# Rows of the first expert pair gathered from DRAM instead of selected on TensorE; sums of the later norms moved to VectorE and GpSimd; two spin counts changed

## The reference

```python
x = _layer_norm(ALPHA * x + gt1 * y, ln_g[l, 0], ln_b[l, 0])
h = x * (1 + sc2) + sh2
y = _hmoe(h, rg_w[l], rg_b[l], re_w[l], re_b[l], exp_wg[l], exp_wu[l], exp_wd[l])
x = _layer_norm(ALPHA * x + gt2 * y, ln_g[l, 1], ln_b[l, 1])

def _hmoe(...):           # comb: weight of each expert for each token, zero but for two
    hid = silu(einsum('nd,edf->nef', xf, wg)) * einsum('nd,edf->nef', xf, wu)
    hid = hid * comb[:, :, None]
    return einsum('nef,efd->nd', hid, wd)
```

## Time and profile before

| | |
|---|---|
| median of three executions | 1046.03 us (1041.26 to 1055.11) |
| the profiled execution, its own time | 1048.08 us |
| its span, first to last instruction | 1046.4 us |
| mean granted TensorE clock | 0.937 of 2.4 GHz |
| TensorE (PE) busy | 917.7 us, 88% |
| VectorE (DVE), ScalarE (ACT), GpSimd (POOL) busy | 31%, 22%, 17% |

### The profile page before, as it was taken

How to read it: one execution, slowest core, us unless ns; L and a number is a source line. 1 busy time by engine, 2 the same in 40 slices (tenths; PEclk the granted TensorE clock), 3 DMA queues, 4 the chain that set the end, 5 groups by cost and what they waited for, 6 DMA issues and landing times.

```text
span 1046.4 us, 19214 instructions
## 1 busy us (share of the span) xinstructions
PE 917.7 (88%) x8268; PEld 627.0 (60%) x8268; DVE 327.6 (31%) x841; ACT 232.0 (22%) x528; POOL 177.2 (17%) x230
## 2 busy tenths in 40 slices
PE   2799999889988989999787899898899989997874
PEld 0477667869876757655354567554467757553442
DVE  0523341535425454211123301221221354211134
ACT  0312225223215041111001332221222131110004
POOL 0100002011542151221031110000000233211122
PEclk9899989999998998999996999899889998999996
DMA  9742221340246931799959454555646724899931
GB/s 385 322 152 89 81 81 48 127 163 4 85 173 271 387 139 57 277 425 423 424 194 369 194 189 179 195 196 214 243 164 234 322 97 182 328 424 421 383 110 46
DMA packets 28773, 230.14 MB, mean 220 GB/s; under 512 B 6590, under 2 KB 7006, under 8 KB 13552
## 3 DMA queue, kind: packets, MB, share of 16 engines
q1 hardware_dynamic: 19200, 208.66, 49.8%
q0 software_dynamic: 7776, 15.50, 4.2%
q10 hardware_dynamic: 1712, 4.75, 1.3%
HBM read 222.16 MB, written 16.32 MB: 228 GB/s over the span
## 4 chain that ended last, share of the span: by engine, by line
PE 68%; DMA 19%; DVE 5%; issue 3%; ACT 2%; POOL 1%; SPq 1%; ACTq 0%; POOLq 0%; DVEq 0%
PE ps L646 21%; PE ps L984 10%; DMA arena<-in_w 8%; DMA arena<-in_experts 6%; PE ps L772 5%; PE ps L667 5%; PE ps L1040 4%; PE ps L628 3%; PE ps L779 3%; DMA arena<-zbuf 2%; PE ps L1005 2%; DMA ring<-in_w 2%; PE ps L1154 2%; PE ps L970 1%; PE ps L925 1%
## 5 line engine op out<-in xcount | busy, mean ns | idle before, releaser
L646 PE MATMUL ps<-arena,ring 128*128 128x288 f32 x896 | 230.9, 420 | 11.5 <-DVE arena L1471 3.8
L646 PEld LDWEIGHTS ps<-arena,ring 128*128 128x128 f32 x896 | 173.9, 196 | 68.9 <-issue 17.1
L984 PE MATMUL ps<-arena 128*64 128x256 f32 x960 | 118.6, 404 | 18.0 <-DMA arena<-in_experts 12.6
L984 PEld LDWEIGHTS ps<-arena 128*64 128x64 f32 x960 | 75.0, 146 | 60.8 <-DMA arena<-in_experts 17.8
L667 PE MATMUL ps<-arena,csil 128*32 128x512 f32 x256 | 40.1, 756 | 36.8 <-DMA arena<-in_w 36.8
L772 PE MATMUL ps<-arena 64*64 64x64 f32 x1888 | 63.8, 221 | 4.3 <-issue 3.2
L772 PEld LDWEIGHTS ps<-arena 64*64 64x64 f32 x1888 | 60.3, 137 | 10.2 <-issue 8.5
L628 PEld LDWEIGHTS ps<-con,arena 128*128 128x128 f32 (+3 forms) x270 | 34.5, 149 | 45.5 <-issue 26.6
L628 PE MATMUL ps<-con,arena 128*128 128x128 f32 (+3 forms) x270 | 52.5, 309 | 10.2 <-DVEq L1737 6.3
L1040 PE MATMUL ps<-arena 128*64 128x512 f32 x208 | 58.4, 598 | 0.8 <-DVE arena L1678 0.8
L2003 ACT ACTIVATE arena<-ps 128x128 f32<-128x128 f32 x36 | 10.0, 277 | 208.8 <-PE ps L984 208.8
(11 more groups left out here) (306 smaller groups left out, 1270.3 us busy)
## 6 DMA issues: line engine op xcount, KB each, us to landing
arena<-in_experts SPq DMA_DIRECT2D x30, 2048.0 KB, 20.6
ring<-in_w SPq DMA_DIRECT2D x24, 2048.0 KB, 8.4
arena<-in_w SPq DMA_DIRECT2D x16, 2048.0 KB, 13.3
arena<-in_experts SPq DMA_DIRECT2D x30, 1024.0 KB, 19.3
ring<-in_experts SPq DMA_DIRECT2D x6, 2048.0 KB, 19.8
ring<-in_experts SPq DMA_DIRECT2D x6, 1024.0 KB, 16.5
arena<-in_lora SPq DMA_DIRECT2D x1, 2560.0 KB, 40.8
hbuf<-arena SPq DMA_DIRECT2D x4, 512.0 KB, 3.2
```

What stands on the lines that cost most here:

```text
L646: last = mm(ps[:, tile % 4, 0:T], wslot[j][:, k, o * P:(o + 1) * P], rhs_at(k), start=k == 0, stop=k == KT - 1)
L984: last = mm(ps[64 * j:64 * j + 64, 2 + b, 0:256], x(k), ewgu[slot][:, k, j * 256:(j + 1) * 256], start=k == 0, stop=k == KT - 1)
```

## The change

Three parts, in both layers.

1. **First pair.** `first_rows` is gone. `fetch(0)` gathers the pair's rows like every other pair's. TensorE runs `tables(0)`, the count, `tables(1)`, `spin(2, 3)`, `step_t(0)` (which waits for the gather), then expert 0; `step_t(1)` moves ahead of expert 1. GpSimd fetches pairs 0 and 1 ahead of `places()` and 2 and 3 behind it. `xsel` moves onto `htok`, `ysel` away from it.
2. **Norms 1 and 3.** VectorE sums the tiles in `residual`, GpSimd the squares, as for norms 0 and 2; TensorE's six products of squares between the transposes become one product with the sum. The addition of the two result rows is split: VectorE adds the first two quarters (after `z_in0`), GpSimd the last two (after `z_in1`, new semaphore `zsum2`).
3. **Spins.** Ahead of the transposes 30 products in place of 24, ahead of K 8 in place of 5.

```diff
@@ TensorE, layer_norm @@
-                if n % 2:
-                    add_squares(n, KT - 2)
                 pe.wait_ge(s["ln_sum"], n + 1)
                 mm(ps[:, 4, 0:T], co("mean"), zsum_, start=True, stop=False)
...
-                if not n % 2:
-                    pe.wait_ge(s["ln_ssum"], n // 2 + 1)
-                    mm(ps[:, 5, 0:T], co("mean"), ssum, start=True, stop=False)
-                add_squares(n, KT - 1).then_inc(s["ln_var"], 1)
+                pe.wait_ge(s["ln_ssum"], n + 1)
+                mm(ps[:, 5, 0:T], co("mean"), ssum, start=True, stop=False)
+                pe.wait_ge(s["ln_sq"], KT * (n + 1))
+                mm(ps[:, 5, 0:T], co("mean"), acts(SQB[n])[:, KT - 1, :], start=False, stop=True)\
+                    .then_inc(s["ln_var"], 1)
@@ TensorE, moe @@
-                pe.wait_ge(s["sel_ready"], 4 * layer + 1)
-                first_rows()
                 tables(0)
...
                 tables(1)
+                spin(2, 3)
+                step_t(0)
                 for e in range(NE):
                     step_u(e)
                     if e < 2:
                         tables(2 + e)
                     if e:
                         step_h(e - 1)
-                    if e == 1:
-                        step_t(1)
-                    if e % 2 == 0 and e:
+                    if e % 2 == 0:
                         if e + 2 < NE:
                             step_t(e // 2 + 1)
-                        step_d(e // 2 - 1)
+                        if e:
+                            step_d(e // 2 - 1)
...
-                spin(6, 24)
+                spin(6, 30)
...
-                        pe.wait_ge(s["zsum"], 4 * layer + k // 2 + 1)
+                        pe.wait_ge(s[("zsum", "zsum2")[k // 4]], 2 * layer + k % 4 // 2 + 1)
...
-                    if k > 1:
-                        add_squares(2 * layer + 1, k - 2)
...
-            spin(6, 5)
+            spin(6, 8)
@@ VectorE @@
-                    if k > 1 and not n % 2:
+                    if k > 1:
                         did(V.tensor_tensor(zsum_, Z[:, 0, :] if k == 2 else zsum_, Z[:, k - 1, :], ALU.add))
...
-                for q in range(4):
+                dve.wait_ge(s["z_in0"], 48 * (layer + 1))
+                for q in range(2):
@@ GpSimd @@
+                if n % 2:
+                    pool.wait_ge(s["z_in1"], 48 * (layer + 1))
+                    for q in range(2, 4):
+                        c = slice(q * 256, (q + 1) * 256)
+                        ch.did(Pl.tensor_tensor(zin[:, 0:2, 0, c], zin[:, 0:2, 0, c], zin[:, 0:2, 1, c], ALU.add))
+                        ch.link(Pl.tensor_tensor(zin[0:TS, 2, 0, c], zin[0:TS, 2, 0, c], zin[0:TS, 2, 1, c], ALU.add))
+                        pool.sem_inc(s["zsum2"], 1)
...
-                for p in range(1, 3):
+                for p in range(2):
                     fetch(p)
                 places()
-                fetch(3)
+                for p in range(2, 4):
+                    fetch(p)
```

More of the change, by code:

```diff
@@ L43 @@
 NSLOT, NPAIR = 5, 8
-GATHERS = (NPAIR // 2 - 1, NPAIR // 2)
 JSLOT = (1, 2)
@@ L411, in build @@
         htok = take(3 * D).rearrange("p (i d) -> p i d", i=3)
-        ysel = [cut(at_rows + n * D, D) for n in range(2)]
-        xselT = [take(D) for _ in range(2)]
-        xsel = [ring[:, ECOL + n * D:ECOL + (n + 1) * D] for n in range(2)]
+        xsel = [cut(at_rows + n * D, D) for n in range(2)]
+        xselT = [cut(at_rows + 2 * D, D), take(D)]
+        ysel = [take(D) for _ in range(2)]
         hsil, hid, hidT = ([take(P) for _ in range(2)] for _ in range(3))
@@ L972, in tables @@
                     last.then_inc(s["sel_mm"], 1)
+                tables(0)
+                for i, n in enumerate(TOK):
+                    last = mm(ps[:, 7, 448:464], ones[0:n, :], mask[0:n, i, :], start=i == 0, stop=i == 2)
+                last.then_inc(s["cnt_mm"], 1)
+                tables(1)
                 def rows_in(x, b):
@@ L999, in moe @@
                 n0, p0 = layer * NE, layer * NPAIR
[L1001 to L1008, removed]
                 def step_t(p):
-                    pe.wait_ge(s[f"gath{p % 2}"], 16 * (layer * GATHERS[p % 2] + (p + 1) // 2))
+                    pe.wait_ge(s[f"gath{p % 2}"], 16 * ((p0 + p) // 2 + 1))
                     for k in range(KT):
@@ L1043, in step_d @@
                     last.then_inc(s["dn_mm"], 1)
-                pe.wait_ge(s["sel_ready"], 4 * layer + 1)
-                first_rows()
-                tables(0)
-                for i, n in enumerate(TOK):
-                    last = mm(ps[:, 7, 448:464], ones[0:n, :], mask[0:n, i, :], start=i == 0, stop=i == 2)
-                last.then_inc(s["cnt_mm"], 1)
-                tables(1)
+                spin(2, 3)
+                step_t(0)
                 for e in range(NE):
@@ L1729, in moe @@
                 scaled_x(2 * layer + 1)
-                for q in range(4):
+                dve.wait_ge(s["z_in0"], 48 * (layer + 1))
+                for q in range(2):
                     c = slice(q * 256, (q + 1) * 256)
-                    dve.wait_ge(s[f"z_in{q // 2}"], 48 * (layer + 1))
                     did(V.tensor_tensor(zin[:, 0:2, 0, c], zin[:, 0:2, 0, c], zin[:, 0:2, 1, c], ALU.add))
@@ L2018, in moe @@
                     step_u(e)
-                    if e == 1:
-                        step_t(1)
-                    if e % 2 == 0 and 0 < e < NE - 2:
+                    if e % 2 == 0 and e + 2 < NE:
                         step_t(e // 2 + 1)
@@ L2195, in layer_norm @@
                 Z, Q, layer = acts(ZB[n]), acts(SQB[n]), n // 2
-                total, x, ready, done = (zsum_, Z, "z_ready", "ln_sum") if n % 2 else (ssum, Q, "ln_sq", "ln_ssum")
+                if n % 2:
[5 more added lines that the diff above has]
+                        pool.sem_inc(s["zsum2"], 1)
                 for k in range(1, KT - 1):
-                    pool.wait_ge(s[ready], KT * n + k + 1)
-                    ch.link(Pl.tensor_tensor(total, x[:, 0, :] if k == 1 else total, x[:, k, :], ALU.add))
-                pool.sem_inc(s[done], 1)
+                    pool.wait_ge(s["ln_sq"], KT * n + k + 1)
+                    ch.link(Pl.tensor_tensor(ssum, Q[:, 0, :] if k == 1 else ssum, Q[:, k, :], ALU.add))
+                pool.sem_inc(s["ln_ssum"], 1)
                 pool.wait_ge(s["ln_mu"], n + 1)
@@ L2246, in fetch @@
                     pool.wait_ge(s["tbl_ready"], 4 * layer + p // 2 + 1)
-                    if p > 2:
+                    if p >= 2:
                         pool.wait_ge(s["xt_mm"], 2 * (p0 + p - 1))
```

5 lines of the change are left out of this document (1 added, 4 removed).

## The result

The changed kernel takes 1038.35 us (median of four executions, 1033.0 to 1040.77), beside 1048.85 us (1041.26 to 1055.11) of the kernel before in the same comparison. The ratio is 0.9894, 95% interval 0.9849 to 0.9939: 11.1 us, or 1.1%, faster (6 to 16 us by the interval), where 12.3 us and a time of 1034 us were forecast. The profiled execution of the changed kernel took 1039.54 us, its span is 1037.8 us and its mean clock 0.932 (0.937 before). All ratios leave out executions that are slow, over 1.5% above the fastest of the same kernel (of e1 three: 1049.2, 1049.4 and 1519.6 us).

A forecast was written before the change was run, and what follows sets the result against it. TensorE was taken to lead the chain of waits (68%, DMA 19%), with experts behind pair 0 at the weights' pace. Gains of 7.0 + 4.8 + 0.5 = 12.3 us from the 1046.03 median gave 1034 us, range 1022 to 1047.

The forecast's parts named there:

- The gather chain (7.6 us): Start of experts: first table, table(0) to gather issue, and landing take 1.70, 1.9 and 4.0 us from the selection matrix.
- The turn ahead of expert 2 at 0.75 us: First pair: turning the hidden rows ahead of expert 2, with its wait, was estimated at 0.75 us.
- First pair together: Selection matrix to end of pair 0's down: 33.2 us plus 0.8 for half clock; gains of 4.2 and 2.9 us.
- The additions at 5.1 us: Rows' return: VectorE's four additions, taking turns with GpSimd's, end after 5.1 us; all eight took 4.66 before.
- The mean at 15.4: Rows' return: mean out 15.4 us after the first addition, against 19.8 and 16.2; gains of 4.4 and 0.8 us.
- 0.2 us late at the variance: Norms 1 and 3: squares' products behind the mean's reach VectorE late, losing 0.2 us each time.
- Norms together, 4.8 us: Norms 1 and 3, both layers: 4.8 us gained; without a collision 0 to 2.8 us more a layer.
- Spins and K, 0.5 us: Longer spins ahead of transposes and K: gain of 0.5 us, between -1.5 and +1.5.
- Kinder ports and clock: Rival: GpSimd and VectorE hardly collide and longer spins hold the clock; 8 us more gained, 1026 us; chance 0.17.
- That the start gains nothing: Rival: the weights bound the start of the experts anyway; 5.3 us remains, 1041 us; chance 0.08.
- The late gather: Rival: the first pair's gather lands late, delaying expert 0 and the weights; 1055 us at the slowest gather; chance 0.08.
- The low clock: Rival: idle TensorE ahead of expert 0 keeps experts 0 to 2 slow, 3 to 5 us a layer; 1042 us; chance 0.15.

The follow-up runs named there:

- e1: The kernel before with part 1 alone (gathered first pair, spin(2, 3), step_t(1) ahead of expert 1), norms and other spins as before; ratio to before 0.9946.
- e4: The changed kernel, but VectorE adds all four quarters of the returned rows again and GpSimd none; ratio to before 0.9860.
- e5: The changed kernel, but GpSimd begins its two quarters only when VectorE has added its own two; ratio to before 0.9869.
- e9: The changed kernel with the late GpSimd additions of e5 and the VectorE order of e7, spin(2, 3) kept; ratio to before 0.9857.
- e6: The changed kernel without spin(2, 3), the three spin products ahead of the first pair's transposes; ratio to before 0.9893.
- e7: The changed kernel, but VectorE copies expert 0's turned hidden rows before it writes table(3); ratio to before 0.9852.
- e2: The kernel before with part 2 alone (tiles summed by VectorE, squares by GpSimd, additions split), spins 24 and 5; ratio to before 0.9957.
- e3: The kernel before with the spins of 30 and 8 alone; ratio to before 0.9980.
- e8: The changed kernel with the edits of e5, e6 and e7 together; ratio to before 0.9860.
- e10: The kernel before with its first_rows, only step_t(1) moved ahead of expert 1 on TensorE and ScalarE; ratio to before 1.0045.

## Why the prediction was right, point by point

**The sum.** 12.3 us forecast, 11.1 measured, and the parts alone gave 5.7, 4.5 and 2.1 (the last within its uncertainty), 12.3 together. Each of these three has an interval of about 4 us to either side, so that their sum meets the forecast as closely as it does is luck. The likeliest case held: about a half each from the first pair and from the return. Inside both halves terms were wrong in either direction, as the points below show, and of the signs named in advance three failed: the gather's landing is not the last wait, expert 0 of layer 1 starts after 11.9 us and not by 11, and the down weights go out slightly after 35.

**The gather chain (7.6 us) plus transposes and copy, expert 0 at 10.1 us.** It started at 10.8 and 11.9. The step that failed is that the tables, the count and the spin "lie beside" the gather: put at 4.1 us with full clock, they took 1.30 + 2.93 + 3.04 = 7.3 us, and outlasted it. The landing took 3.5 and 3.4 us (4.0 taken), so the gather was through 1.9 and 2.1 us before the transposes began, and the chain that I named as the last wait wasn't it. The half clock that the earlier trace rows show at the tables was not applied to the products that I placed beside the gather; `tables(1)` takes the same 2.93 us in the chain of the kernel before:

```profile
409.01 2.93 PE ps L970 x12
```

Three more profiles of the same program (layer 0 of e4, e5 and e9) have expert 0 at 12.3 us: there `tables(0)` already takes 2.3 us.

**Expert 0 at 6.0 us.** It took 3.67 in layer 0 and 5.34 in layer 1. I had taken the clock of the kernel before; the spin changes it (e6).

**The turn ahead of expert 2 at 0.75 us.** 1.47 us, since on VectorE `table(3)` stands ahead of the copy (e7). I had looked at the order of TensorE and not at what VectorE does before the answer.

**First pair together.** 34 us forecast; 35.4 and 35.2 measured. Over all kernels the old order has 38.3, 37.1, 38.4, 35.4, 38.5 and 37.1 (before, e2, e3), mean 37.5, the new one with its spin and without other edits of this stage 35.4, 35.2, 32.4, 35.2, 35.3, 32.4, 34.9 and 35.5 (after, e1, e4, e5), mean 34.6. So 2.9 us a layer, 5.8 in all, where 7.0 were forecast. The two profiles alone give 4.8. Against the terms of the forecast (which had 0.8 us a layer set aside for half clock), in the changed kernel expert 0 of layer 0 starts 0.7 us late, expert 1 takes 1.3 us more, the turn 0.7, expert 2 1.8, and expert 0 takes 2.3 us less. In layer 1 expert 0 starts 1.8 us late, the turn takes 0.7 us more and expert 0 0.7 less. That the total comes near is partly luck: the spin's effect on expert 0, which I hadn't foreseen, paid for other terms.

**The additions at 5.1 us.** They ended after 5.0, with the residual at 5.12 and 5.18: right, and for the reason given. When VectorE and GpSimd both add in SBUF, each waits for the other's instruction to end. e5 removes the overlap and the 1.54 us fall to 0.69. The rule of the Trainium skill, page "SBUF — State Buffer", section "SBUF: two separate sides", that the second of the two engines is fully blocked on the port pair, agrees with this.

**Tiles of 1.27 us.** 1.25, and the last residual starts after 14.1: right.

**The mean at 15.4.** 16.4 and 16.1: the step that was mis-sized is "1.0 us for the mean's last product". Both products stand behind VectorE's last sum (L908 waits for it), 1.33 + 0.96 us at half clock. In the kernel before both stood on the chain too, behind two products of squares:

```profile
572.22 2.22 PE ps L925 x4
574.43 0.96 PE ps L914 x2
575.39 0.85 PE ps L916 x2
```

**0.2 us late at the variance.** The root is 5.47 us behind the mean, against 4.71 before, so 0.8. The products give 0.1 to 0.2. Another 0.5 is VectorE's small operation L1497, 0.97 us where the old kernel has 0.44: it begins while a subtraction of GpSimd (2.79 us for three, from 573.74) is running and ends with it. In the kernel before it began about where one of them ended and the next began. This is read from the timelines, and no run was made for it, but four other profiles of the new return bear it out (layer 0 of e5, layer 1 of e2, e8 and e9). There the last product of squares ends sooner, the same operation begins 2.27 us behind the mean's copy and not 2.49, takes 0.42 us, and the root is 4.71 us behind the mean (4.70 in e2).

**Norms together, 4.8 us.** To the root, the two profiles give 2.6 in layer 0 and -0.7 in layer 1. The old return has its root at 24.5, 20.9, 20.4, 20.0, 24.4, 23.5, 21.2 and 23.4 us (before, e1, e3, e10), mean 22.3; the new one at 21.9, 21.6, 21.8, 20.3, 21.7, 21.3, 21.9 and 21.3 (after, e2, e6, e7), mean 21.5. So 0.8 us a layer on average; with the clock low it is 3 us better, with the clock high up to 1.5 us worse. What part 2 mainly does is take the clock out of this stage. The rest of its worth is in K, whose first tile takes 4.7 us in every kernel with it, against 5.77 to 6.93 without: 1.0 to 2.2 us. That is 2.6 to 3.8 us by the stages; the times of e2 give 4.5, with an interval that holds both. So the forecast gain of 4.8 us is not contradicted, but its split is: 0.8 us was forecast for layer 1, where the root comes 0.7 us later.

**Spins and K, 0.5 us.** K's first tile is 1.1 us shorter, but for part 2 (e2 has it with the spin of 5). The spins alone show nothing (e3).

**The rivals.** Kinder ports and clock fell: the ports collide in full. That the start gains nothing fell: from the down weights' issue to the return it is 119 to 121 us in after and 120.3 and 120.5 in before, and 118.5 to 122.4 in all kernels, though the issue comes anywhere from 32.4 to 50.4 us after the matrix. So an earlier or later issue moves the whole stream. The late gather fell (3.5 us). The low clock came true in part, with expert 0 of layer 1 at 5.34 and expert 2 of layer 0 at 5.36 us, and accounts for a part of the first pair's shortfall in layer 0. In layer 1 expert 0 was quicker than forecast, and the shortfall is its late start and the turn. Where both experts ran at full clock and expert 0 started after 10.8 us (e1 in layer 0, e4 in layer 1) the stage takes 32.4 us; in layer 0 of e5 both ran at full clock too, but with a start at 12.3 us and a slow expert 1 it takes 34.9.

**Open.** In layer 0 of the changed kernel expert 1 takes 4.9 us, with gaps of 0.05 to 0.34 us that the profile puts down to nothing; in layer 1 and in e1 it takes 3.6. In both layers of e5, e7 and e9 it is 4.3 to 5.1. What these gaps are was not tried.

## What to carry to other kernels

Work moved from TensorE to VectorE and GpSimd should not run on both of them at the same time if all operands of both lie in SBUF: let one begin when the other is through (2.34 us against 5.1 to the first residual here, 1.3 us to the mean), or leave it whole. When products are placed beside a transfer, count them at the clock that the stretch really has; and when a wait is added or removed on one engine, read in the order of the engine that answers what stands ahead of the answer.

## What the runs showed of the hardware

- Three products of 288 columns, 3.0 to 3.2 us at half clock, mostly decide how long the expert behind them takes: with them 3.67 us in ten of twelve layers (after, e1, e4, e5, e7, e9; 5.34 and 5.35 in the other two), without them 5.53 to 6.59 in the four of e6 and e8. TensorE was busy with narrow products (6 and 16 columns) right before them, at 0.50.
- The same 24 products took 8.51 us at a granted clock of 1.00 in one kernel and 14.75 us at 0.51 in another (e10), from the same place in the program.
- GpSimd's additions of 128x512 take 1.26 us where GpSimd began first, while VectorE's beside them go from 0.69 to 1.54; GpSimd's small one goes from 0.71 (e5) to 1.16. The engine that was first lost nothing; each later instruction ends as if it had waited for the other engine's. Once VectorE was first, in layer 1 of e2, and there GpSimd lost 0.5 us (timelines of VectorE and GpSimd):

```profile
1019.88 0.69 DVE L1727 TENSOR_TENSOR arena<-arena 128x512 f32<-128x512 f32 x1 [0.15 <-DVE arena L1728]
1019.94 1.75 POOL L2194 TENSOR_TENSOR arena<-arena 128x512 f32<-128x512 f32 x1 [0.50 <-POOL arena L2195]
```

- VectorE's residual, which has one input in PSUM, takes 0.65 us beside GpSimd's addition (e5) and 0.64 without one (before).
- The gather of the first 128 rows of 4 KB lands 3.3 to 3.5 us after its issue (after, e6, e8). In the changed kernel the DMA engines' busy share is 0.00 when it is issued (404.1 to 405.4).
